# The second group's page choice ahead of the rotated retention keys, its exponentials between two copies, in a one-core hybrid decoder step

## What is computed

```python
rq, rk, rv, rg, mq, mk, mv = split(rmsnorm(x) @ w_in)          # 7 blocks of 512 columns
rq, rk = rotary(rq), rotary(rk) * RET_DK ** -0.5                # 4 retention heads of 128
ret_o, state = retention_chunked(rq, rk, rv, s0, chunk)         # decayed queries and keys
# attention of 8 heads: each query takes its own block and the 3 past blocks (of 256) with the
# highest mean score, softmax over these
gate = q @ mean(k_block);  top_i = top_k(gate, 3);  p = softmax(where(mask, q @ k * scale, -inf))
mix = concat(groupnorm(ret_o) * silu(rg), p @ v)
h = x + mix @ w_out
y = rmsnorm(h + moe(rmsnorm(h)))                                # top 4 of 32 experts, clamped SwiGLU
```

## Time and profile before

| | before |
|---|---|
| time, median of 3 runs | 1238.06 us (1237.89 to 1240.36) |
| span of the profiled execution | 1237.4 us |
| the profiled execution's own time | not shown; the span is 0.7 us under the median |
| PE busy | 1197.3 us, 97% |
| DVE, ACT, POOL busy | 382.1, 239.5, 68.3 us |
| DMA | 500.64 MB, mean 405 GB/s; 8 or 9 tenths busy in 39 of 40 slices |
| a transfer of cached values | 10.4 us from issue to landing (median of 16) |

### The profile page before, as it was taken

How to read it: one execution, slowest core, us unless ns; L and a number is a source line. 1 busy time by engine, 2 the same in 40 slices (tenths; PEclk the granted TensorE clock), 3 DMA queues, 4 the chain that set the end, 5 groups by cost and what they waited for, 6 DMA issues and landing times.

```text
span 1237.4 us, 17275 instructions
## 1 busy us (share of the span) xinstructions
PE 1197.3 (97%) x7264; PEld 508.4 (41%) x7264; DVE 382.1 (31%) x555; ACT 239.5 (19%) x560; POOL 68.3 (6%) x70
## 2 busy tenths in 40 slices
PE   6999999999999999999999999999999999999997
PEld 3455544635443434344343434344343434343432
DVE  4999955434311111221111111122111111111122
ACT  4021144504111101121111101021111111110103
POOL 2222202230000000000000000000000000000000
PEclk9999999999999999999999999999999999999999
DMA  8999889999899999999999999999999999999995
GB/s 335 384 361 363 331 331 383 365 384 389 365 421 427 428 427 427 431 427 430 427 430 429 427 431 426 431 427 430 428 427 430 427 430 427 429 429 427 428 427 209
DMA packets 49978, 500.64 MB, mean 405 GB/s; under 512 B 5656, under 2 KB 6320, under 8 KB 19088
## 3 DMA queue, kind: packets, MB, share of 16 engines
q1 hardware_dynamic: 42416, 430.56, 83.2%
q0 software_dynamic: 7520, 69.47, 14.2%
HBM read 495.29 MB, written 4.72 MB: 404 GB/s over the span
## 4 chain that ended last, share of the span: by engine, by line
PE 66%; DMA 21%; DVE 7%; issue 4%; ACT 2%; SPq 0%; DVEq 0%; ACTq 0%
PE psum L1028 24%; DMA arena<-w_gate_up 18%; PE psum L1059 14%; DVE arena L1582 6%; PE psum L936 6%; DMA arena<-w_down 3%; PE psum L956 3%; PE psum L534 3%; PE psum L942 2%; PE psum L754 2%; PE psum L968 2%; PE psum L625 2%; PE psum L454 2%; PE psum L975 1%; PE psum L1095 1%
## 5 line engine op out<-in xcount | busy, mean ns | idle before, releaser
L1028 PE MATMUL psum<-arena 128*64 128x512 f32 x1920 | 421.7, 594 | 11.6 <-DMA arena<-w_gate_up 11.5
L1028 PEld LDWEIGHTS psum<-arena 128*64 128x64 f32 x1920 | 135.0, 137 | 294.6 <-issue 267.8
L1931 DVE TENSOR_SCALAR arena<-psum 128x512 f32<-128x512 f32 x32 | 22.2, 692 | 675.1 <-PE psum L1028 635.7
L1059 PE MATMUL psum<-arena 128*64 128x512 f32 x960 | 212.6, 595 | 0.0
L1185 ACT ACTIVATE arena<-psum 128x512 f32<-128x512 f32 (+3 forms) x190 | 96.2, 509 | 350.3 <-PE psum L1059 170.7
L1582 DVE STREAM_TRANSPOSE arena<-arena 128x2048 f32<-128x2048 f32 x32 | 121.2, 3940 | 2.0 <-PE psum L519 1.9
L1059 PEld LDWEIGHTS psum<-arena 128*64 128x64 f32 x960 | 66.2, 137 | 124.3 <-issue 122.5
L534 PE MATMUL psum<-arena 128*128 128x512 f32 x224 | 107.3, 616 | 0.4 <-ACT arena L1185 0.4
L1455 ACT ACTIVATE arena<-arena 128x512 f32<-128x512 f32 x30 | 18.9, 631 | 412.4 <-DVE arena L1931 412.4
L1185 ACT ACTIVATE arena<-psum,arena 128x128 f32<-128x128 f32 (+2 forms) x162 | 49.1, 401 | 173.6 <-PE psum L534 113.4
L936 PE MATMUL psum<-arena 128*128 128x128 f32 x512 | 76.9, 293 | 0.2 <-DVE arena L1843 0.2
(11 more groups left out here) (264 smaller groups left out, 712.1 us busy)
## 6 DMA issues: line engine op xcount, KB each, us to landing
arena<-w_gate_up SPq DMA_DIRECT2D x128, 2048.0 KB, 31.0
arena<-w_down SPq DMA_DIRECT2D x63, 2048.0 KB, 32.9
arena<-w_in SPq DMA_DIRECT2D x7, 2048.0 KB, 18.4
arena<-w_out SPq DMA_DIRECT2D x2, 2048.0 KB, 12.9
out<-arena POOLq DMA_DIRECT2D x1, 2048.0 KB, 19.8
arena<-w_down SPq DMA_DIRECT2D x2, 1024.0 KB, 38.8
out<-arena SPq DMA_DIRECT2D x3, 512.0 KB, 3.3
arena<-x_prompt SPq DMA_DIRECT2D x2, 512.0 KB, 5.4
```

Source lines behind the costliest of these rows:

```text
L1028: last = mm(psum[64 * g:64 * (g + 1), b, :], xt[:, 2 * kk + m, lhs], gate_slot[slot][:, m, c:c + 512], start=False, stop=kk == 3 and m == ...
L1059: last = mm(psum[64 * g:64 * (g + 1), 2, :], at_sb[:, m, SLOTS * q:SLOTS * (q + 1)], down_slot[slot][:, m, 512 * g:512 * (g + 1)], start=q ...
```

## The change

On DVE `choose(1)` moves from behind the division of the prompt's probabilities to the place ahead of the rotation of the keys, and the rotation of the keys with the decayed queries moves behind the copy of sequence 1. On ACT `probabilities(1)` moves from behind the copy of the prompt's attention output to the place between the two prompt tiles of the last projection block. No operation is added or taken away.

```diff
@@ ACT
             ins.then_inc(p_exp, 1)
             evacuate_sequence(0)
             evacuate_block(z_rg)
+            probabilities(1)
             evacuate_block(z_rg, 1)
             evacuate_sample(z_rg[0:NS, 2, :])
             evacuate_sequence(2)
@@
             A.emptied(copy(mix_t[:, 4:6, 0:LP], psum[:, A.bank(), :].rearrange("p (c w) -> p c w", c=2)))
-            probabilities(1)
             evacuate_pt(1, 0)
             evacuate_pt(1, 1)
@@ DVE
             v.tensor_scalar(pm[:, 16:32], pm[:, 0:16], -SCALE, None, ALU.mult).then_inc(p_bias, 1)
-            rotate(rot_k, mark["z4"])
-            qd = const("q_dec").rearrange("p (t h) -> p t h", t=TILES)
-            kd = const("k_dec").rearrange("p (t h) -> p t h", t=TILES)
-            v.tensor_tensor(q_dec, rot_q[:, 1:3], qd[:, 1:3].unsqueeze(3).broadcast_to([P, 2, RH, P]),
-                            ALU.mult).then_inc(qdec_ready, 1)
+            choose(1)
             dve.wait_ge(p_exp, 1)
             link(v.reciprocal(pm[:, 48:64], pm[:, 32:48]))
@@
                 .then_inc(p_probs, 1)
-            choose(1)
             evacuate_sequence(1)
+            rotate(rot_k, mark["z4"])
+            qd = const("q_dec").rearrange("p (t h) -> p t h", t=TILES)
+            kd = const("k_dec").rearrange("p (t h) -> p t h", t=TILES)
+            v.tensor_tensor(q_dec, rot_q[:, 1:3], qd[:, 1:3].unsqueeze(3).broadcast_to([P, 2, RH, P]),
+                            ALU.mult).then_inc(qdec_ready, 1)
             for u in range(1, 6, 2):
                 evacuate(pt_prompt[:, 4 * u:4 * u + 4, :].rearrange("p b t -> p (b t)"))
```

## The result

The change made the kernel slower. It takes 1245.87 us (median of 16 runs, 1240.37 to 1251.46), the kernel before, on the same chip beside it, 1238.72 us (16 runs, 1237.1 to 1240.36): ratio 1.0057, 95% interval 1.0044 to 1.007, or 7 us lost where 3.3 us of gain were forecast. It lies outside the range. Two of the 16 runs took 1240.4 and 1240.7 us, hardly more than the slowest of before, so the loss need not come in every execution. The profiled execution took 1248.08 us, its span is 1246.3 us, against 1237.4 us of before.

What follows compares the result with a forecast made beforehand. It took PE to set the start of the weight transfers that set the end. The 1.4 us of idle time and a halved low-clock stretch made 3.3 us off, from 1238.06 to 1234.8 us, range 1233.6 to 1238.2.

Steps and rivals of the forecast that it cites:

- Does it reach the end: From the transposes at 213.28 us to the kernel's end: an earlier PE starts the expert weight stream equally earlier.
- (1): DVE's page choice moved ahead to 181.63 to 188.5 us, fitting before the reciprocal with 0.4 us to spare: cost 0.
- (2): DVE's rotation and decayed queries behind the copy of sequence 1, ending at 200.3 us, 3.0 us to spare: cost 0, gain 0.
- (3): ACT's exponentials between the last block's two copies: 4.3 us, ending at 194.3, 4.4 us to spare; no moved step issues DMA.
- (4): PE goes from value set 7 at 211.86 us straight into the transposes: 1.4 us of idle time goes for certain.
- (5): PE's low clock from 215.4 to 222.0 us halves to 3.3 us, making the whole shift some 3.3 us, not 1.4.
- A: The forecast case: idle time gone, slow stretch after 213 us halved or gone, 2.5 to 4.1 us gained, 1234.8 us; chance 0.47.
- rival B: Only the idle time goes, the clock after 213 us stays low as long as before: 1236.6 us; chance 0.34.
- (6): Transfers from 224 to 314.70 us: retention state lands at 230.7, 1.1 us to spare after a 3.3 us shift, cap 4.4.
- Rival C: Nothing arrives: loads at the expert stage end at about 316.2 us regardless, or another wait replaces the removed one: 1237.7 us; chance 0.13.
- Rival D: Slower: low clock in 224 to 300 us grows by more than 2.8 us over PE's moved work: 1240.0 us; chance 0.06.

Runs made afterwards that it cites:

- changed again: The changed kernel with no edit, run for a second profiled execution: 1246.05 us, ratio 1.0058 to the kernel before.
- router held: Changed kernel with the two loads of the router's weights and bias issued only when the retention state has landed: 1244.44 us, ratio 1.0042.
- quarter early: Changed kernel with the retention state's sequences 6 and 7 loaded apart and ahead, once value set 5 is through: 1243.86 us, ratio 1.0027.
- before again: The kernel before with no edit, run for a second profiled execution: 1240.16 us, ratio 0.9999.
- DVE half: Changed kernel with DVE's new order kept and ACT's exponentials put back in their old place: 1237.91 us, ratio 0.9989 to the kernel before.
- two and four added matmuls: Changed kernel with filler matmuls, their result unread, behind value set 7: two 1238.49 us, ratio 0.9987; four 1240.42 us, ratio 1.0004.
- three kernels: Changed kernel with value transfer 11 held until the state landed: alone 1246.28 us, with router loads held too 1245.44, with the state's last quarter early 1246.25.

## Why the prediction was wrong

The profiled executions whose landing the trace shows, by the distance between the two issues:

| distance, us | kernels | state's landing, us | PE then waits |
|---|---|---|---|
| 13.0 | changed, changed again, router held, quarter early | 28.4, 26.4, 29.9, 30.2 | 5.2 to 9.1 us, L786 |
| 14.5 to 16.8 | before, before again, DVE half, two and four added matmuls, transfer 11 a set later | 20.6, 20.2, 20.5, 20.4, 21.0, 20.3 | not at L786 |
| 19.6 to 21.7 | transfer 11 held until the landing (three kernels) | 20.9, 20.1, 18.7 | 2.5 to 6.3 us, L625 |

The state's load is issued when the prompt's output is through, ahead of the idle time that the change removes. Transfer 11 is issued when set 8 is through, behind it. Taking 1.4 us out between them brings the two issues 1.5 us closer, 13.0 for 14.5 us, and that is over an edge. What happens on it, in the queues of the changed kernel (packets, MB, share), first from 223 to 225 us, with a value transfer in flight, then from 227 to 231 us, between transfers 10 and 11:

```profile
q0 software_dynamic: 45, 0.74, 90.6%
q1 hardware_dynamic: 44, 0.09, 11.8%
```

```profile
q1 hardware_dynamic: 565, 1.16, 100.5%
q0 software_dynamic: 9, 0.03, 2.1%
```

Beside a value transfer the state gets as many packets as it, 44 and 45. But its packets are of 2 KB (0.09 MB / 44) and the values' of 16 KB (0.74 MB / 45), so it gets a ninth of the bytes (0.09 of 0.83 MB). The Trainium skill ("DMA: Bandwidth & Descriptors", Queues, rings and completion order) says that each DMA engine takes turns between the queues that have work, a whole packet at a time; the trace agrees with its 45 and 44. The state comes in the quiet stretch, 0.29 MB a microsecond, and what has not come when transfer 11 fills the engines again crawls behind it.

Now the steps of the prediction.

**Does it reach the end: right.** A shift at the transposes is handed on, also when it is a loss: 7.03 us at the first gate matmul, 6.9 at the end of the span.

**(1) and (2), DVE's order: right.** The choice starts when the scores are there and takes 185.64 to 192.63. The reciprocal still waits for the prompt's exponentials (line 1333), not for the choice, and DVE is idle for 3.21 us ahead of the next copy. All are 4 us later than forecast, as PE was already in that execution.

**(3), ACT's order: right.** The exponentials and the own-token one run from 193.84 to 198.1, 4.3 us as summed, and the second copy waits for PE alone, with 4.55 us to spare for 4.4.

**(4), 1.4 us of idle time go for certain: right in its place.** The chain shows PE going from set 7 to the transposes without a gap, and set 6 to set 8 takes 1.48 us less than in the second profile of before.

**(5), the clock: the term was mis-sized, 1.9 us for 0.** I took the low stretch of one execution for a consequence of what stood ahead of it, and put half of it into the sum. The second profile of before and the DVE half have the same idle time and a granted clock of 1.00 behind it. The text named the weakness itself (no row showed two executions, and the Trainium skill, "TensorE: Matmul & The Clock Gate", Part 1: the HAM clock gate, says that the point of the change differs) and still let the sum rest on it. The size of the stretch was read well: full clock was to be worth 2.5 us there, and the two profiles of before differ by 2.3 (line 640 takes 1.04 us at full clock for 0.94 forecast, line 637 gains 0.36 for 0.1, the transposes take 5.05 for 4.7). It was not the change's to win. The sign set for A, a mean clock of 0.75 or more between 213 and 222 us, was met with 1.00; the second profile of before has 1.00 as well, so it could not tell A from no change. Without this term the forecast would have been 1236.6 us, rival B, and still wrong by its sign.

**(6), the transfers on the way: this step failed.** It took the landing as a duration, 20.6 us from the issue, and set 4.4 us as the cap of any shift. A shift of 1.5 us was therefore three times covered. But the 20.6 us hold only while transfer 11 keeps away, and transfer 11 is one of the things that the shift moves. The landing went to 26.4 to 30.2 us. The step looked at who waits for the load, and not at who shares the engines with it. Step (3) had settled the transfers with "No DMA is issued by any moved step": true, but a step that issues none can still move the issues of another engine.

**The rivals.** Rival C had "another wait takes the place of the one removed" with the loads of the values as a candidate, but priced at no gain. Rival D had the right sign and another mechanism. It decided once the low clock from 224 to 300 us grew by more than 2.8 us. That sign was met: the trace's clock is low there for 3.4 us before (269.9 to 273.3) and for 10.2 us after (237.9 to 248.1), and the fall near 270 us is gone. But the new low stretch begins inside the 7.28 us wait, as it does in the changed kernel again (237.6, in a wait from 235.4 to 240.6). It costs 1.94 us in lines 786 and 790 (0.30 + 1.64), and the first gate matmul gets 0.9 us back. The loss is the wait.

**The end of the load.** The landing moves by 6 to 10 us for 1.5 us of distance. Where they are spent can be read from the trace's single events, which no view prints. The state's semaphore counts to 16, and the trace has 16 updates of it. I take each for the share of one of the 16 DMA engines; that is an inference, since the trace names no engine. With the router held 15 updates come from 230.96 to 232.79 us and the last at 242.95. In the changed kernel 13 come by 232.97, the others at 234.60, 236.74 and 242.54. With the early quarter 15 of the larger part's come by 233.12 and the last at 243.14. In the second profile of before all 16 lie between 232.10 and 234.16. The queues with the router held, from 233 to 242 us:

```profile
q0 software_dynamic: 259, 3.74, 99.5%
q1 hardware_dynamic: 13, 0.03, 0.8%
```

259 packets are 16 for each engine, so the state's 13 are about the turns of a single engine. They start 0.72 us apart; a value packet takes 0.62 us there and one of the state's 0.08, where the state's take 0.12 us each in the quiet stretch. By these times a dozen packets left on one engine when transfer 11 reaches it need some 8.6 us in place of 1.4 (an estimate). It need not be one engine alone: in the changed kernel again six of the 16 updates come after 233.1 us.

**What stays open.** Why so little decides. The packets of transfer 11 first appear 17.3 to 17.4 us behind the state's issue in the changed kernel, its second profile and the router's run, and 17.2 to 17.8 us in the second profile of before, the DVE half and two added matmuls: hardly anything of the 1.5 us between the issues is left there. What differs is how fast they spread: 18.5 us behind the state's issue 14 or 15 value packets are under way at once in the first three and 8 to 12 in the others. Why that is so, why an engine lags, and whether it is always the same one is not shown. Nor is it shown that 13.0 us in other executions always means a late landing.

## What to carry to other kernels

The state's time from issue to landing was no property of its transfer, but of what shared the DMA engines meanwhile (18.7 to 30.2 us). Before moving the work that starts transfers, write down for each pair in flight which event issues it, and see whether the change moves one and not the other. Where small packets ran beside large ones, the small ones got their turn and not their bytes, so a load of 2 KB packets that must be early wants its quiet stretch, and it is the big transfer's issue that has to be kept away (here by one value set, 2.8 us). And a clock stretch seen in one execution is not to be put into a sum before a second execution shows it.

## What the hardware did that was not expected

- 1.5 us of distance between two issues made 6 to 10 us of landing. The other way, 2.8 us more of it took 8 us off the kernel.
- The state alone in its quiet stretch moves 1.16 MB in 4 us, 290 GB/s, against 408 GB/s with the value transfers running; issued behind the prompt's output, it landed in no trace sooner than 18.7 us, even with transfer 11 held back and a quarter of it gone.
- TensorE's granted clock was 0.50 for 6.6 us in one execution of the kernel before and 1.00 at the same place, behind the same 1.4 us of idle time, in another and in the DVE half. Behind 7.28 us of idle time it was 0.50 (line 790: 3.57 us for 1.93), and behind waits of 3.6, 6.3 and 2.5 us for values as well, where it cost 6.0, 2.1 and 5.0 us in the three groups that followed: after the shortest of these waits twice as much as the wait itself.
- The gain of 1.5 us is real in the chain, and no version was shown to be faster than the kernel before: the best, 0.9987 with intervals up to 1.0001 and 1.0002, all still hold 1.
